# A joint attention and recurrence stage on one Trainium2 core: its written-out order planned from other numbers, with a short patience for TensorE's array shape

## What is computed

```python
def nsa_mixer(...):                     # 8 heads of 64, blocks of 128 queries
    ...
    p_c = masked_softmax(s_c, cmp_end[None, :] <= t[:, None])     # 63 compressed keys
    ...
    p_s = masked_softmax(s_s, pos_s <= t[:, None])                # with 16 blocks and top 16: all causal keys
    ...
    p_w = masked_softmax(s_w, (pos_w[None, :] >= 0) & (rel >= 0) & (rel < WINDOW))
    return gb[..., 0:1] * o_c + gb[..., 1:2] * o_s + gb[..., 2:3] * o_w

def rwkv7_mixer(...):                   # 8 heads of 64, a recurrence over 1024 tokens
    def step(state, inp):
        sa = jnp.einsum('bhvk,bhk->bhv', state, -kk_t)
        state = (state * w_t[:, :, None, :] + sa[..., None] * (kk_t * a_t)[:, :, None, :]
                 + v_t[..., None] * k_t[:, :, None, :])
        return state, jnp.einsum('bhvk,bhk->bhv', state, r_t)
```

## Time and profile before

| what | us |
|---|---|
| three runs, median | 2499.07 |
| the profiled execution, its own time | 2501.89 |
| its span, first to last instruction | 2500.1 |
| joint stage, first to last matmul | 1068.1 to 1510.0 |

### The profile page before, as it was taken

One profiled execution on the slowest core, in us unless ns is written; L12 is line 12 of the kernel. 1 busy time (PEld: TensorE's weight loads), 2 busy tenths in 40 slices (PEclk: granted clock), 3 DMA queues, 4 the chain that ended last, 5 costly groups with the idle time before them and its releaser, 6 DMA issues. The chain is left out here.

```text
span 2500.1 us, 46924 instructions
## 1 busy us (share of the span) xinstructions
PE 2464.7 (99%) x19328; PEld 2018.4 (81%) x19328; DVE 1671.6 (67%) x2492; ACT 1048.5 (42%) x1827; POOL 191.6 (8%) x212
## 2 busy tenths in 40 slices
PE   8999999999999999999999999999999999999999
PEld 7888888888877778977888877877788888888887
DVE  6976676678654474567877778634458776676676
ACT  4422322355443353456666564523343322323443
POOL 0000000000000000034454430000000000000000
PEclk9999999999999999989999999999999999999999
DMA  4223323654442358942212116501122323326464
GB/s 153 96 89 122 115 78 119 236 184 151 139 134 62 101 159 258 241 124 57 53 47 57 33 45 236 178 8 34 68 76 97 127 67 122 125 68 219 139 201 149
DMA packets 281163, 297.79 MB, mean 119 GB/s; under 512 B 75483, under 2 KB 211864, under 8 KB 280984
## 3 DMA queue, kind: packets, MB, share of 16 engines
q1 hardware_dynamic: 279976, 294.33, 37.7%
q10 hardware_dynamic: 1008, 0.92, 0.1%
HBM read 208.57 MB, written 81.36 MB: 116 GB/s over the span
## 5 line engine op out<-in xcount | busy, mean ns | idle before, releaser
L1246 PE MATMUL f_ps<-hi,f_wh 128*128 128x512 f32 x656 | 255.6, 390 | 0.8 <-DVE f_wl L930 0.8
L1248 PE MATMUL f_ps<-hi,f_wl 128*128 128x512 f32 x656 | 255.2, 389 | 0.0
L2900 PE MATMUL f_ps<-hi,f_ahead_h 128*128 128x512 f32 x384 | 160.0, 417 | 0.8 <-PEq L72 0.8
L1246 PE MATMUL f_ps<-f_t3h,f_t2h 128*128 128x512 f32 x392 | 152.5, 389 | 0.0
L1247 PE MATMUL f_ps<-f_t3l,f_t2h 128*128 128x512 f32 x392 | 152.5, 389 | 0.0
L1248 PE MATMUL f_ps<-f_t3h,f_t2l 128*128 128x512 f32 x392 | 152.5, 389 | 0.0
L2902 PE MATMUL f_ps<-hi,f_ahead_l 128*128 128x512 f32 x384 | 150.0, 390 | 0.0
L2901 PE MATMUL f_ps<-one_lo,f_ahead_h 128*128 128x512 f32 x384 | 149.8, 390 | 0.0
L1246 PEld LDWEIGHTS f_ps<-hi,f_wh 128*128 128x128 f32 x656 | 123.2, 188 | 27.1 <-issue 1.7
L1248 PEld LDWEIGHTS f_ps<-hi,f_wl 128*128 128x128 f32 x656 | 123.2, 188 | 25.5
L1247 PE MATMUL f_ps<-one_lo,f_wh 128*128 128x512 f32 x344 | 133.9, 389 | 0.0
(11 more groups left out here) (639 smaller groups left out, 6586.1 us busy)
## 6 DMA issues: line engine op xcount, KB each, us to landing
act<-one_y SPq DMA_DIRECT2D x30, 512.0 KB, 3.6
f_work<-act SPq DMA_DIRECT2D x30, 512.0 KB, 3.6
act<-y SPq DMA_DIRECT2D x30, 512.0 KB, 3.5
arena<-act SPq DMA_DIRECT2D x30, 512.0 KB, 3.7
one_y<-in_w_in SPq DMA_DIRECT2D x25, 512.0 KB, 4.0
early<-in_ffn_w_gate SPq DMA_DIRECT2D x11, 1024.0 KB, 6.2
early<-in_ffn_w_up SPq DMA_DIRECT2D x11, 1024.0 KB, 8.7
f_raw<-in_ffn_w_gate SPq DMA_DIRECT2D x10, 1024.0 KB, 6.3
```

What stands on the lines that cost most here:

```text
L1246: nc.tensor.matmul(out, wh, xh, start=start, stop=False)
L1248: return nc.tensor.matmul(out, wl, xh, start=False, stop=stop)
L2900: nc.tensor.matmul(dense_ps[:, b, cols], w_hi[:, b, k, :], hi[:, k, cols], start=(k == 0), stop=False)
```

## The change

The plan of the joint stage gets other durations for nearly all events. From an event's end to its readers it counts 0.1 us (`NEAR`) in place of 0.2 (`HOP`), and VectorE's and ScalarE's durations are multiplied by 0.86 (`OVERLAP`). A change of TensorE's shape counts 0.15 us in place of 0.1. New is a patience: if nothing of the present shape is ready for TensorE, but something of it will be within 0.15 us (`PATIENCE`), the plan lets TensorE wait for it. The four masked tiles of the levels become an event of their own for every chunk, which may stand behind other work of GpSimd. No instruction is added or taken away, and none changes its shape.

```diff
--- before.py
+++ after.py
@@ -1507,11 +1507,13 @@
 
 
 STRAIGHT = {"tf", "gr"}
-ON_PE = {"gram_b": 0.7, "tf": 0.47, "gr": 0.92, "s": 0.7, "out": 0.7, "var": 0.25, **{f"t{lv}": 0.24 for lv in range(LEVELS - 1)}}
+ON_PE = {"gram_b": 0.7, "tf": 0.47, "gr": 0.93, "s": 0.7, "out": 0.7, "var": 0.33, **{f"t{lv}": 0.235 for lv in range(LEVELS - 1)}}
 OUT_OF = {"gram_b": 1.1, "gram_k": 0.7, "tf": 0.42, "gr": 0.84, "s": 0.43, "out": 0.75, "var": 0.47,
           **{f"t{lv}": 0.42 for lv in range(LEVELS - 1)}}
 WIDE = {"gram_b", "gram_k", "wu", "gr"}
 HOP = 0.2
+NEAR = 0.1
+OVERLAP = {"dve": 0.86, "act": 0.86}
 ISSUE = 0.61
 
 
@@ -1531,7 +1533,8 @@
 
 
 STAY = 10.0
-TURN_AROUND = 0.1
+TURN_AROUND = 0.15
+PATIENCE = 0.15
 
 
 def in_order(engine, takes, needs, lag=None, tiling=None):
@@ -1563,6 +1566,13 @@
             ready[engine[e]][e] = 0.0
     while any(ready.values()):
         at, eng = min((max(free[g], min(r.values())), g) for g, r in ready.items() if r)
+        if eng == "pe" and tiled:
+
+            same = [x for x in ready[eng] if tiled[x] == now]
+            soon = [ready[eng][x] for x in same if ready[eng][x] <= free[eng] + PATIENCE]
+            if soon and not any(ready[eng][x] <= at for x in same):
+                free[eng] = max(free[eng], min(soon))
+                continue
         e = max((x for x, t in ready[eng].items() if t <= at), key=lambda x: rank[x] + STAY * (x in tiled and tiled[x] == now))
         del ready[eng][e]
         plan.append(e)
@@ -1593,18 +1603,19 @@
         u, k = s // 4, s % 4
         n = u // PAIRS + 1 if k < 2 else min(u // PAIRS + 1, 5)
         us, extra = 0.001 * n * P, 0.2 * (k >= 2)
-        event(("score", s), "pe", 0.113 * n + 0.1, s and ("max", s - 1))
-        event(("max", s), "dve", 0.25 + 1.1 * us + extra, ("score", s), u >= 2 and ("bank", FIRST_FILL[u - 1] - 1))
-        event(("exp", s), "act", 0.4 + us + 2 * extra, ("max", s), s and ("exp", s - 1))
+        groups = [min(n - m, 4) * P for m in range(0, n, 4)] if k < 2 else ([(n - 1) * P] if n > 1 else []) + [P + NB + 1]
+        event(("score", s), "pe", 0.09 + sum(2 * max(w / 2400 + 0.0137, 0.109) for w in groups), s and ("max", s - 1))
+        event(("max", s), "dve", 0.31 + 1.04 * us + 1.5 * extra, ("score", s), u >= 2 and ("bank", FIRST_FILL[u - 1] - 1))
+        event(("exp", s), "act", 0.49 + 0.84 * us + 2.65 * extra, ("max", s), s and ("exp", s - 1))
         if k % 2:
-            event(("scale", s), "dve", 0.45 + (1.3 * us if k == 1 else 0.35), ("exp", s), s > 1 and ("scale", s - 2))
+            event(("scale", s), "dve", 0.95 + 1.14 * us if k == 1 else 0.78, ("exp", s), s > 1 and ("scale", s - 2))
         if k == 3:
-            event(("window", s), "pool", 0.3 + 3.0 * us, ("scale", s))
+            event(("window", s), "pool", 0.65 + 5.1 * us, ("scale", s))
     for n, (u, f) in enumerate(FILLS):
         m = len(turns(u)[f])
-        event(("bank", n), "pe", 0.115 * len(places(turns(u)[f])), ("scale", last_step(u, f)), last_step(u, f) % 4 == 3 and ("window", last_step(u, f)), n and ("copy", n - 1))
-        event(("copy", n), "act" if n % 2 else "dve", 0.1 + 0.125 * len(places(turns(u)[f])), ("bank", n), n >= 2 and ("values", n - 2))
-        event(("values", n), "pe", 0.22 * m, ("copy", n), n and ("values", n - 1), 
+        event(("bank", n), "pe", 0.109 * len(places(turns(u)[f])), ("scale", last_step(u, f)), last_step(u, f) % 4 == 3 and ("window", last_step(u, f)), n and ("copy", n - 1))
+        event(("copy", n), "act" if n % 2 else "dve", (0.14 if n % 2 else 0.12) + (0.112 if n % 2 else 0.14) * len(places(turns(u)[f])), ("bank", n), n >= 2 and ("values", n - 2))
+        event(("values", n), "pe", 0.215 * m, ("copy", n), n and ("values", n - 1), 
               f == 0 and u and ("finish", u - 1), f == 0 and u and u % PAIRS == 0 and ("tile_ms", u // PAIRS - 1))
         if n + 1 == FIRST_FILL[u + 1]:
             i = u // PAIRS
@@ -1623,16 +1634,15 @@
 
             before = {"gram_b": [out_of("var", c - 2)],
                       "yt0": [out_of("ax"), ("masked", c)],
-                      "yt1": [out_of("t0"), ("levels", c) if c < 2 else ("masked", c)],
+                      "yt1": [out_of("t0"), ("levels", c)],
                       "s": [out_of("gr"), out_of("s", c - 1)],
                       "var": [("square", c)]}.get(name, [n and out_of(PRODUCTS[n - 1])])
             event(("rw", c, name), "pe", ON_PE.get(name, 0.47), *before)
             event(("out_of", c, name), "dve" if name in TO_DVE else "act", OUT_OF.get(name, 0.58), ("rw", c, name),
                   name == "s" and c and ("rw", c - 1, "out"))
             if name == "gram_b":
-                event(("masked", c), "pool", 4.6 if c >= 2 else 2.0, out_of(name))
-                if c < 2:
-                    event(("levels", c), "pool", 2.8, ("masked", 1), ("out_of", 1, "gram_k"), c and ("levels", 0))
+                event(("masked", c), "pool", 2.4, out_of(name))
+                event(("levels", c), "pool", 3.1, ("masked", c), *([("masked", 1), ("out_of", 1, "gram_k"), c and ("levels", 0)] if c < 2 else []))
             if name == "out":
                 event(("square", c), "act", 0.4, out_of(name))
             if name == "var":
@@ -1655,7 +1665,8 @@
 
         return e[0] == "values" and "columns" or e[0] == "rw" and (e[2] != "var" or not crossed(e[1])) and "corners" or "whole"
 
-    return in_order(engine, takes, needs, tiling=tiling)
+    takes = {e: us * OVERLAP.get(engine[e], 1.0) for e, us in takes.items()}
+    return in_order(engine, takes, needs, dict.fromkeys(needs, NEAR), tiling)
 
 
 def window_keys(hi):
@@ -1970,8 +1981,6 @@
                     op(j, LTm[j][:, 0], GB[j][:, :, 0, :], over_pairs(m_lev[:, 0, :]), ALU.mult)
                     pool.wait_ge(by_pool[j], through(gn, c, "one"))
                     op(j, T0[j][:], T0[j][:], over_pairs(eye[:]), ALU.add)
-                    if c >= 2:
-                        levels(c)
                     if c == 0:
 
                         pool.wait_ge(decay_in, 32)
```

## The result

The changed kernel takes 2507.36 us (median of six runs, 2503.94 to 2510.00), the one before 2499.07 (six runs): a ratio of 1.0035, 95% interval 1.0026 to 1.0045. It is **slower by 8.3 us**, more than the 5 us that a measurement can tell from no change, and inside the range on record. The profiled execution took 2503.94 us by its own time, the shortest of the six.

A forecast was written before the change was run, and what follows sets the result against it. The prediction took TensorE, in flight for 99% of 2500.1 us, as the bound. Its terms, -16.0 - 1.5 + 15.2 + 5 = +2.7 us on the 2499.1 us median, gave 2501.8 us; range 2490 to 2510.

The forecast's parts named there:

- the second rival, VectorE: Joint stage: VectorE becomes the bound, a reciprocal ahead of a `copy` stops TensorE; +10.5 us, 2509.6 us; chance 0.28.
- 1, fewer changes of shape: Joint stage on TensorE: 531 changes of shape become 431, 100 at 0.16 us; 16.0 us saved, bounds 12 and 17.
- 2, `window` ahead: GpSimd in the joint stage: `window` no longer stands behind four masked tiles; 1.5 us saved, between 0 and 3.
- 3, shorter cover: Joint stage: grouping removes work between producer and reader, 71 short places against 18; 15.2 us lost, bounds 10 and 17.
- 4, queues on VectorE, ScalarE: Joint stage: some `copy` and `max` steps start late behind other work; 5 us lost, bounds 0 and 11.
- the 112 further places: Joint stage: places with less than 0.5 us to spare rise from 132 to 244; 0.045 us lost at each.
- the point of decision: Queue cost in the joint stage from which the slower VectorE rival decides: 0.065 us a place.
- the 132 places: Joint stage, order before: places with less than 0.5 us to spare, said to cost next to nothing.
- the walk's ways: Joint stage, group by group, each product to its reader without queues: short by 4.0 us before, 19.2 now.
- What would show it: Joint stage signs: "issue" pauses shrink about 15 us, waits grow from some 5 to 20 or 25, stage 442 within 5.
- the slower course: Joint stage: slower by over 5 us, chance 0.33 together; sign: waits over 30 us and a stage of 452.
- The rival of the clock: Joint stage: new waits lower TensorE's clock; three stretches at 0.66 make the sum +7.8, 2506.9 us; chance 0.05.

The follow-up runs named there:

- the best order: Changed kernel planned with 0.25 us to a reader, VectorE 1.08, ScalarE 1.12, GpSimd 0.94 times, a patience of 0.26 us; 2491.09 us, ratio 0.9970.

## Why the forecast's sum was too low

The forecast was 2501.8 us, with a chance of 0.50 for a sum within 5 us of no change; it came out on the side of the second rival, VectorE, which stood at 2509.6 with 0.28. The measured time lies in the range only because that rival set its upper end. Term by term, whole stage:

| term | forecast | measured | from |
|---|---|---|---|
| 1, fewer changes of shape | -16.0 | -13.2 | 100 at 0.132 |
| 2, `window` ahead | -1.5 | -1.1 | GpSimd's queue 1.1 to 0.0 |
| 3, shorter cover | +15.2 | +10.6 | ways 4.6 to 15.2 |
| 4, queues on VectorE, ScalarE | +5 | **+12.7** | 3.2 to 15.9 |
| sum | +2.7 | +9.0 | runs: +8.3; stage at full clock: +9 to +12 |

*Term 4 failed*, by 7.7 us. I took 0.045 us for each of the 112 further places with little to spare; it is 12.7 / 112 = 0.11, beyond the 0.065 that I gave as the point of decision and a little above the upper bound of 0.1. The step behind it was to price the new places by the old ones ("the 132 places cost next to nothing"). Even these were not free: their queues come to 3.2 us, 0.024 each; the forecast had set the waits in the rows against the walk's ways alone. What the rows show is that in the order after late steps on VectorE follow one another: at 1364 to 1368 us `scale`, `max` and the `copy` behind it are all asked for at once. A rate counted where such steps stand apart does not hold there. The Trainium skill, "TensorEngine Tiling (Array Packing)", section Performance Considerations, says that the PSUM copy may become the bottleneck after a fourfold speedup of TensorE by tiling. Here the shapes are the same in both orders, so the rule bears on it only in kind, and so far the trace agrees: VectorE's queue, 14.1 us for 3.0, though VectorE is busy for no longer (240.9 us of the stretch for 241.8). Part of that queue is `scale`, which takes nothing out of PSUM.

*Term 3* was right in kind and too large by 4.6, near its lower bound of 10. A place that is short by its way and late by a queue was counted in both terms, which may be the reason; no run tells it.

*Term 1*: the price of 0.16 came from all pauses of PEld over all changes. Between the last matmul of a group and the first of the next I count 0.20 us at most changes and 0.15 behind a product of the recurrence with 64 columns; but 0.10 stay between two `values`, where there is no change. In the stretch 75 changes fewer saved 9.9 us, 0.132 each, near the lower bound of 0.12.

The errors cancel in part: terms 1 and 4 came out 2.8 and 7.7 us above the forecast, term 3 4.6 below it.

*What would show it*: PEld's pauses for "issue" shrank by 13 us, near the 15 forecast, but that is luck, for in the stretch, at equal clock, they shrank by 3.6. The waits were to grow from some 5 to 20 or 25; in the view that the forecast named they come to some 15 us for PE and 25 for PEld, while late starts came to 31 us (14.1 + 1.8 + 15.2) where 8.9 were before, and over 30 was the sign of the slower course. The stage at 445.2 lay within 5 of 442, but only because the clock gave 6 to 8.5 us back. These signs could not tell what they were meant to. The rival of the clock did not come: all of the changed order's 3.4 us at 1.2 GHz lie at the stage's start. It is not empty, though: without the patience one fall inside the stage followed a wait of 2.98 us.

## What to carry to other kernels

A planner's durations must be those that a reader sees, from the product's end to the reader's start, with room for what queues on the engine between; numbers that are too short fill TensorE on paper and leave it standing on the chip. When an order gets tighter, the queue of the engine that takes results out is to be priced by walking the order with every engine's work in sequence, not by the rate of the looser order. And before two traces are compared, the granted clock of each stretch is to be read: here it hid some 6 to 8.5 us of a growth of 9 to 12.

## What was not expected of the chip

The clock differs from execution to execution of one kernel: 0.996 to 0.999 of full speed in the changed kernel's six. At the stage's start TensorE was at 1.2 GHz for 17.0 us in the trace before, 3.4 after, 10.2 in the best order's; one trace of each order does not tell whether the order plays a part.

What separates two groups on TensorE is a few fixed steps rather than a spread. From a group's last matmul to the first of the next, the median over the traces is 0.04 us between products of the recurrence with 64 columns, 0.10 between two `values`, 0.15 or 0.20 at a change of shape, with another 0.05 in the first round behind it.

And `scale` on VectorE is held up while GpSimd works: with GpSimd idle no step of it was lengthened, beside GpSimd's masks one of 0.16 us took up to 4.19.
